# A norm turned unscaled, by quarters, beside the projection ahead of it: the token's scale is applied to the products instead

## The reference

```python
x = x + mixed @ w_out                        # the projection, 2048 x 2048
xn = rms_norm(x, norm2_g)                    # x * rsqrt(mean(x*x) + eps) * g
qh = (xn @ peer_w_q).reshape(T, 8, 2, 128)   # queries
sub = einsum("thpc,hpnc->thpn", qh, sub_keys)   # key scores
v1, i1 = top_k(sub[:, :, 0], 16); v2, i2 = top_k(sub[:, :, 1], 16)
vals, cidx = top_k(all sums v1 + v2, 16)     # 16 experts of 16384 per head
gates = softmax(vals)
h = xn @ u_sel.T ;  a = gelu(h) * gates ;  y = a @ v_sel
```

## Time and profile before

| | |
|---|---|
| median of 3 runs | 3324.85 us (3324.84 to 3324.94) |
| the profiled execution, its own time | 3327.32 us |
| its span | 3325.5 us |
| granted clock, mean | 0.995 of full |
| PE busy | 3255.3 us (98%) |
| DVE busy | 2281.4 us (69%) |
| ACT busy | 1550.7 us (47%) |
| DMA | 590.51 MB, mean 178 GB/s |

### The profile page before, as it was taken

How to read it: one execution, slowest core, us unless ns; L and a number is a source line. 1 busy time by engine, 2 the same in 40 slices (tenths; PEclk the granted TensorE clock), 3 DMA queues, 4 the chain that set the end, 5 groups by cost and what they waited for, 6 DMA issues and landing times.

```text
span 3325.5 us, 52769 instructions
## 1 busy us (share of the span) xinstructions
PE 3255.3 (98%) x20926; PEld 2875.0 (86%) x20926; DVE 2281.4 (69%) x3250; ACT 1550.7 (47%) x1988; POOL 5.6 (0%) x14
## 2 busy tenths in 40 slices
PE   7999999999999999998999999999999999999999
PEld 6999999888888888887789999888888888888887
DVE  5664445677577567788659997578787577865554
ACT  4554344555355455554544544444343444434453
POOL 0000000000000000000000000000000000000000
PEclk9999999999999999998999999999999999999999
DMA  6545565655556655552445554554555655555555
GB/s 230 159 146 193 187 209 185 203 190 194 192 179 195 195 187 176 181 168 77 143 155 165 171 172 141 184 171 150 188 177 184 188 185 178 182 186 190 190 190 165
DMA packets 161253, 590.51 MB, mean 178 GB/s; under 512 B 17904, under 2 KB 18064, under 8 KB 159728
## 3 DMA queue, kind: packets, MB, share of 16 engines
q1 hardware_dynamic: 160192, 583.14, 54.5%
q0 software_dynamic: 816, 3.98, 0.3%
HBM read 584.96 MB, written 2.10 MB: 177 GB/s over the span
## 4 chain that ended last, share of the span: by engine, by line
PE 90%; DVE 7%; ACT 2%; issue 1%; DMA 0%; DVEq 0%; SPq 0%; ACTq 0%
PE PS L410 19%; PE PS L368 12%; PE PS L370 12%; PE PS L369 12%; PE PS L413 10%; PE PS L378 7%; PE PS L379 7%; PE PS L380 7%; DVE LO L294 2%; PE PS L1456 1%; DVE GB L1071 1%; PE PS L1467 1%; PE PS L717 0%; ACT UN L672 0%; ACT HI L293 0%
## 5 line engine op out<-in xcount | busy, mean ns | idle before, releaser
L294 DVE TENSOR_TENSOR LO<-RAW,HI 128x1024 fp32r<-128x1024 f32 x1096 | 1327.6, 1218 | 770.3 <-ACT HI L293 768.0
L293 ACT ACTIVATE HI<-RAW 128x1024 fp32r<-128x1024 f32 x1096 | 1150.5, 1055 | 1176.0 <-PE PS L370 606.8
L410 PE MATMUL PS<-XX,HI 128*128 128x512 f32 x2688 | 735.5, 395 | 0.0
L368 PE MATMUL PS<-HI,FH 128*128 128x512 f32 x1632 | 644.1, 395 | 5.8 <-DVE FL L584 5.4
L370 PE MATMUL PS<-HI,FL 128*128 128x512 f32 x1632 | 636.9, 390 | 0.0
L378 PE MATMUL PS<-XX,HI 128*128 128x256 f32 x2176 | 624.1, 287 | 12.2 <-DVE LO L294 9.4
L369 PE MATMUL PS<-LO,FH 128*128 128x512 f32 x1632 | 635.7, 390 | 0.0
L379 PE MATMUL PS<-XX,HI 128*128 128x256 f32 x2176 | 616.3, 283 | 0.0
L380 PE MATMUL PS<-XX,LO 128*128 128x256 f32 x2176 | 616.1, 283 | 0.0
L410 PEld LDWEIGHTS PS<-XX,HI 128*128 128x128 f32 x2688 | 459.6, 189 | 61.9
L413 PEld LDWEIGHTS PS<-XX,LO 128*128 128x128 f32 x2688 | 412.4, 189 | 57.2
(11 more groups left out here) (274 smaller groups left out, 2267.8 us busy)
## 6 DMA issues: line engine op xcount, KB each, us to landing
RAW<-in_peer_v SPq DMA_DIRECT2D x256, 512.0 KB, 4.0
RAW<-in_ffn_w_up SPq DMA_DIRECT2D x176, 512.0 KB, 4.3
RAW<-in_peer_ut_rest SPq DMA_DIRECT2D x160, 512.0 KB, 3.9
RAW<-in_w_in SPq DMA_DIRECT2D x136, 512.0 KB, 3.7
RAW<-in_peer_ut SPq DMA_DIRECT2D x96, 512.0 KB, 3.5
RAW<-in_ffn_w_down SPq DMA_DIRECT2D x88, 512.0 KB, 4.3
RAW<-in_w_mix_out SPq DMA_DIRECT2D x32, 512.0 KB, 4.3
RAW<-in_w_in_2c SPq DMA_DIRECT2D x32, 512.0 KB, 4.1
```

The lines of the kernel that those rows point to most:

```text
L293: hi_done.append(AC.do(lambda e, raw=raw, hi=hi: e.activation(hi, raw, ACT.Copy), landed[i], used))
L294: lo_done.append(DV.do(lambda e, raw=raw, hi=hi, lo=lo: e.tensor_tensor(lo, raw, hi.bitcast(F32), ALU.subtract), hi_done[i], landed[i], used))
L368: e.matmul(o, x, hi[:, k, :], start=f, stop=False, skip_group_check=True)
L410: e.matmul(o, hi[:, k, w], XX[:, 4 * u + k, :, :].rearrange("p h s -> p (h s)"), start=u == 0 and k == 0, stop=False, skip_group_check=True)
```

## The change

The residual is turned unscaled as at w_mix_out: each quarter of the projection calls `turned`, so the multiplication by g, the transposes and the split of quarters 0 to 2 are laid between the units of the following group, and those of quarter 3 behind the first unit of the query product. `scale_of` still runs after the fourth quarter; its y multiplies the key scores in the copy to SUB (ACT, one number per token and so per partition), and `spread` puts it as a row R3 for the up products. These multiply by R3 on DVE: in `up_staged` two DVE multiplications per group read PSUM and write where the gelu wrote before, and the gelus then work in place; in `product_both`, since `late` is no longer empty, one more DVE multiplication per call (40 calls).

```diff
+    RD3 = over("RD3", [128, 2, 128], 33 * K)
...
     for g in range(4):
         pair, banks, m = product(True, 8, FH, FL, lambda k: conv_ready[k // 4])
-        acc_free[pair] = residual(banks, m, g, True, m_res)
-
-
-    x_ready, m_un, m_un_read = normed(scale_of(4, m_ssq[0]), GB, m_gb, m_x_read)
+        acc_free[pair] = marks = residual(banks, m, g, True, m_res)
+        if g == 0:
+            peer_marks, m_un, m_un_read = [None] * 4, [], []
+        evacuations.append(turned(g, GB, [marks, m_ssq[0]], m_gb, m_x_read, peer_marks, m_un, m_un_read))
+    advance(evacuations)
+    x_ready = lambda k: peer_marks[k // 4]
+    y3, m_y3 = scale_of(4, m_ssq[0])
+    R3 = CONST[:, CONSTS["cos"][0]:CONSTS["cos"][0] + S]
+
+    def third_spread():
+        yield
+        yield
+        late.append((R3, spread(y3, m_y3, RD3[:], R3, conv_ready)))
+        yield
+
+    beside.append(third_spread())
...
             d = SUB[:, t, 4 * g:4 * g + 4, :]
-            t_free[i] = AC.do(lambda e, b=b, d=d: e.activation(d, b.rearrange("p (k s) -> p k s", k=4), ACT.Copy), m,
-                              conv_ready, box2["pt_read"], box2[1])
+            t_free[i] = AC.do(lambda e, t=t, b=b, d=d: e.activation(
+                d, b.rearrange("p (k s) -> p k s", k=4), ACT.Copy, scale=y3[:, t:t + 1]), m, m_y3, conv_ready,
+                box2["pt_read"], box2[1])
...
             pair, banks, m = product(False, 16, XH, XL, x_ready)
-            acc_free[pair] = m1 = [AC.do(lambda e, i=i, j=j, b=banks[i]: e.activation(
-                dst[:, 4 * j + 2 * i:4 * j + 2 * i + 2, :], two(b), ACT.Gelu), m, free) for i in range(2)]
+            r, m_r = late[0]
+            acc_free[pair] = m0 = [DV.do(lambda e, i=i, j=j, b=banks[i], r=r: e.tensor_tensor(
+                dst[:, 4 * j + 2 * i:4 * j + 2 * i + 2, :], two(b), r.unsqueeze(1).to_broadcast([128, 2, S]), ALU.mult),
+                m, m_r, free) for i in range(2)]
+            m1 = [AC.do(lambda e, i=i, j=j: e.activation(
+                dst[:, 4 * j + 2 * i:4 * j + 2 * i + 2, :], dst[:, 4 * j + 2 * i:4 * j + 2 * i + 2, :], ACT.Gelu), m0[i])
+                for i in range(2)]
             staged.append(m1)
```

## The result

| | before | after |
|---|---|---|
| median | 3324.97 us | 3332.52 us |
| lowest and highest of 14 runs | 3324.09 to 3326.88 | 3331.82 to 3333.46 |
| ratio after to before, 95% interval | | 1.0022 (1.0015 to 1.0029) |
| profiled execution, its own time; span | 3327.32; 3325.5 | 3332.25; 3330.5 |
| DVE busy | 2281.4 | 2317.4 |

The change makes the kernel 7.55 us slower, 0.23%. That is just over the 0.2% that the prediction took as its bound, and the interval (0.15 to 0.29%) lies on both sides of it. Forecast were 6.4 us more than before and 3331.3; it became 3332.5.

The account below looks back on a forecast made before the run. PE bounds the kernel, except from 1860 to 1978, where DVE's uninterrupted queue sets the pace. Boundary -9.3 plus up products +15.7 gives +6.4 us, a predicted median of 3331.3, range 3320.5 to 3337.

Parts of the forecast that it names:

- The boundary: Between the projection's last matmul and the query product's first: 13.5 us lost today, 4.2 afterwards, so 9.3 us gained.
- the 13.5 of today's cost: PE time lost around the norm, between projection and query product, in the kernel before: 13.5 us, slow clock included.
- Per group 2.9 us of DVE: At each up-product group's end: two multiplications 1.29, then DVE waiting on ACT's gelu and HI before LO; 2.9 us altogether.
- The stretch: DVE's uninterrupted queue holding the ends of g0 to g5: 6 x 2.9 = 17.4, less 1.7 idle filled, 15.7 us lost.
- g6 to g11 and the 40 later multiplications: Later up products, where PE is the bound: nothing lost; at most 6 us for the groups and 3 for `product_both`.
- The scale in the copy to SUB: Key scores' copy to SUB: a per-token scale costs nothing, since it is the same instruction.
- PE's shortfall: PE's time not busy in the stretch where DVE sets the pace: from 6.6 us now to 20 or more.
- Rival 1: Up products: gelus waiting for DVE don't hold up the next LO, only durations count; 6.0 less 9.3, 3321.6; 12%.
- Rival 2: Up products: DVE's additions are absorbed and the boundary's gain of 9.3 stays; 3315.6; 7%.
- Rival 3: Ends of g1 to g4: new waits slow PE's clock, four falls cost 6.8; 3338.1, or 3334.7 if half; 17%.
- the prediction's own case: Whole kernel: DVE sets the stretch's pace, so a clock fall costs nothing; 3329 to 3334; 60%.
- Rival 4: Projection: DVE or g holds the early quarters, PE waits, up to 5 of the 9.3 are lost; 3336; 4%.

Follow-up runs that it names:

- the norm alone: The change without any multiplication of the up products (gelus read PSUM unscaled, later up products unscaled): 3317.14 us, ratio 0.9976 to the kernel before.
- the multiplications alone: The change with the old norm put back and all multiplications by R3 kept: 3340.32 us, ratio 1.0048 to the kernel before.
- The wait alone: The change with its 24 multiplications in g0 to g11 replaced by one-column DVE memsets that the gelus wait for: 3328.72 us, ratio 1.0012 to the kernel before.
- prepare first: The change with the next unit's HI and LO queued ahead of each group's multiplications and gelus: 3324.22 us, ratio 0.9999 to the kernel before.
- the norm with the later ones: The change without the 24 multiplications in g0 to g11, keeping the 40 in `product_both`: 3317.50 us, ratio 0.9974 to the kernel before.
- Twice the work: The change with each of the 24 multiplications in g0 to g11 done twice: 3345.25 us, ratio 1.0058 to the kernel before.

## Why the prediction was right, point by point

- **The boundary, 9.3 forecast, 9.0 by the trace.** By the trace its terms hold one by one. Three quarters on PE: forecast 2.7, measured 0.83 + 1.85 = 2.7 between units 536 and 551. Quarter 3's wait and transposes: forecast 1.2, measured from 1698.98 + 0.12 to 1700.38, 1.28. The row R3: forecast 0.3, measured 0.36 between units 554 and 555. By the medians the norm alone gave 7.5, and that is the better measure: the 13.5 of today's cost was read from a single execution, 2.5 above the median, and the 9.0 is measured against the same one. The prediction counted both of its slow stretches (0.8 for the second); the multiplications alone, with one of them, are 1.0 faster over the same norm. The boundary was so put too high by up to 1.8. About 0.5 between trace and medians stay unexplained; the kernel before spreads over 3 us in its runs.
- **Per group 2.9 us of DVE.** Measured 1.28 for the pair and 1.64 to 1.65 for the wait, against 1.29 and 1.61. This was the step that decided the sign, and it came from reading two queues side by side, not from durations. The wait alone (11.6) and prepare first (8.3 back) show both halves separately.
- **The stretch, 15.7 forecast, 15.8 by the trace, 15.4 and 15.6 by the medians** (change over the norm alone; multiplications alone over before). The number of groups that fall into the stretch, six, held: one more or fewer would be 2.9. DVE's first cast of the gates (L1401 before) stands at 1972.48, forecast 1974. The difference of 1.5 is the 1.85 of the first line in the table, less 0.3 by which the shift is otherwise larger than forecast.
- **g6 to g11 and the 40 later multiplications, nothing forecast, nothing found**: the shift is constant from unit 640 on, and the norm with the later ones is 0.4 above the norm alone.
- **The scale in the copy to SUB "costs nothing, since it is the same instruction"**: wrong in itself, and without effect. The eight copies take 0.69 each with the scale of one number per token, 0.60 without it, 0.7 us of ACT in all. ACT waits for PE ahead of them (7.8 in all), so the time doesn't show it.
- **PE's shortfall "20 or more"** was put too high: it is 16.7, and 1.4 more in the window ahead of it. By the loss of 15.8 on top of the old 6.6 it would be 22.4. Of the 4.3 missing, 3.4 is PE at half clock twice, some 3.4 us each, in which it counts as busy while it does half the work; 0.9 is not accounted for.
- **Rival 1, only durations count**: fallen. The wait that it denies is in the trace six times. As an edit (prepare first) it exists, and then costs 7.1 (6.7 by the trace) where it had 6.0. It took all 1.7 of DVE's idle time at the end as filled; in the edit 1.13 of it is still there, at 1960.17.
- **Rival 2, absorbed**: fallen, 15.4 us are not absorbed.
- **Rival 3, the clock falls**: half right and without effect on the time. The new waits did bring the clock to half rate, twice, some 3.4 us each. In that the Trainium skill's rule, as the prediction named it, is now seen on waits of this kind too. But the stretch lost 15.8 where DVE's queue alone gives 15.7, and up to the gates DVE has no wait but the six that the multiplications bring, so the falls cost nothing: PE had more slack to DVE than they took. That is the argument of the prediction's own case. Twice the work shows its edge, in the one fall just ahead of matmuls for which DVE then waits.
- **Rival 4, late quarters**: fallen; between the projection's groups PE is full, and quarter 3 waits 0.27.

The sum, 6.4 (0.19%), was 1.1 below the medians' 7.55 (0.23%). In the traces no term was off by more than 0.3; by the medians the stretch was right (15.4 for 15.7) and the boundary too high (7.5 for 9.3). The mechanism and its size were foreseen. That the result fell on the slower side of 0.2%, by 0.9 us, was luck: the forecast of 6.4 itself lies just below that bound of 6.65, and the chances of 0.48 and 0.44 say as much.

## What to carry to other kernels

When a step moves from an engine that waits for PE to one that is itself behind, look at what is queued behind the waiting instruction on the first engine: here a gelu that waits for DVE kept back a weight conversion that DVE needed next, and this mutual wait cost more (1.65 a group) than the work moved (1.28). Queue the look-ahead work first, or better, let the engine that only waits for PE empty PSUM unscaled, and apply the scale in the next stage in which the busy engine has room: this kept the whole gain of 7.5 us that the change as made turned into a loss of 7.5.

## What the runs showed of the hardware that I had not expected

- GpSimd's elementwise work is paid by DVE. While a POOL multiplication of 128x512 in SBUF ran, DVE's LO went from 1.22 to as much as 2.36 and the mean of a 128x32 operation from 0.18 to 0.40 (L1340 over 1810 to 1985). By the trace six pairs cost 7.4 us on DVE's path, where the same six pairs on DVE itself cost 6.7 without the wait.
- A half-rate stretch of TensorE need not cost anything: two of 3.4 us in the change left no mark on the unit starts behind the stretch, because DVE set the pace in it, and with twice the work three that make 17 us left none either. Where PE sets the pace such a stretch costs about half its length: at 1307.0 to 1310.4 in the kernel before PE is busy throughout and does 9 matmuls where the kernel after does 16, and it costs 1.6.
- The same norm, in two profiles of kernels that have it, had two half-rate stretches in one and one in the other, and differed by 1.0 us. A gap that is priced from one profiled execution carries this with it.
